# Six matmul widths instead of five in an expert loop, and its code on a block boundary

## What is computed

```python
logits = (xt @ router_w + router_b)                  # 1024 tokens x 32 experts
top_val, top_idx = lax.top_k(logits, 4)              # each token goes to 4 experts
# for the tokens of expert e (xb), in blocks:
gu  = xb @ w_gu[e] + b_gu[e]                         # 1024 -> 2048
act = glu * sigmoid(1.702 * glu) * (lin + 1)         # from the two halves of gu, clamped
y   = act @ w_down[e] + b_down[e]                    # 1024 -> 1024
# y times the token's gate is added to the token's row
```

```
139 138 60 61 114 114 145 77 129 120 134 122 117 149 116 80
80 128 217 110 143 174 181 168 118 161 168 117 108 184 156 68
```

## Time and profile before

| | |
|---|---|
| median of 3 executions | 2286.57 us (2285.47 to 2297.29) |
| profiled execution, its own time | 2288.99 us |
| its span, first to last instruction | 2287.2 us |
| TensorE matmul busy | 2216.6 us, 97% of the span |
| matmuls of the expert loop (L1031) | 1563.1 us busy, 12,288 of them |
| mean granted TensorE clock | 0.986 of full speed |

### The profile page before, as it was taken

How to read it: one execution, slowest core, us unless ns; L and a number is a source line. 1 busy time by engine, 2 the same in 40 slices (tenths; PEclk the granted TensorE clock), 3 DMA queues, 4 the chain that set the end, 5 groups by cost and what they waited for, 6 DMA issues and landing times.

```text
span 2287.2 us, 40244 instructions
## 1 busy us (share of the span) xinstructions
PE 2216.6 (97%) x14694; PEld 1904.5 (83%) x14695; DVE 1412.9 (62%) x2880; ACT 570.8 (25%) x1248; POOL 259.4 (11%) x237
## 2 busy tenths in 40 slices
PE   8999999999987999999999999999999999999996
PEld 4444554556667999999999999999999999999996
DVE  3442231577765687768767767764765566667567
ACT  2122221344401222222222222221222222222123
POOL 1000000021141011001101110010110010000013
PEclk9999999999988999999999999999999999999998
DMA  8000002111145899989989889885987788788788
GB/s 310 33 0 1 0 1 74 72 56 57 47 142 187 266 313 300 311 272 316 314 278 304 293 261 318 303 284 188 316 252 235 238 264 291 247 289 297 236 253 295
DMA packets 244509, 486.79 MB, mean 213 GB/s; under 512 B 24552, under 2 KB 24760, under 8 KB 244428
## 3 DMA queue, kind: packets, MB, share of 16 engines
q1 hardware_dynamic: 223532, 450.36, 56.7%
q0 software_dynamic: 20704, 35.60, 7.2%
q10 hardware_dynamic: 224, 0.16, 0.0%
HBM read 475.57 MB, written 49.61 MB: 230 GB/s over the span
## 4 chain that ended last, share of the span: by engine, by line
PE 92%; DVE 4%; issue 2%; ACT 1%; DMA 1%; POOL 0%; DVEq 0%; SPq 0%; POOLq 0%; ACTq 0%
PE PS L1031 65%; PE PS L662 15%; PE PS L858 5%; PE PS L798 1%; PE PS L831 1%; DVE pairA L1807 1%; PE PS L820 1%; PE PS L743 1%; PE PS L740 0%; PE PS L877 0%; DVE unit L1536 0%; PE PS L635 0%; DVE pairA L1853 0%; PE PS L698 0%; DMA unit<-h_dram,cur_x 0%
## 5 line engine op out<-in xcount | busy, mean ns | idle before, releaser
L1031 PE MATMUL PS<-pairA,unit 128*128 x12288 | 1563.1, 290 | 32.9 <-issue 29.1
L1031 PEld LDWEIGHTS PS<-pairA,unit 128*128 128x128 f32 x12288 | 1554.6, 191 | 41.6 <-issue 41.0
L1788 DVE STREAM_TRANSPOSE unit<-unit 32x512 f32<-32x512 f32 (+1 forms) x512 | 325.5, 636 | 10.9 <-DMA unit<-h_dram,cur_x 3.7
L1807 DVE STREAM_TRANSPOSE pairA<-unit 32x512 f32<-32x512 f32 (+1 forms) x512 | 325.8, 636 | 7.1
L662 PE MATMUL PS<-pairA,unit 128*128 128x512 f32 (+1 forms) x528 | 233.6, 598 | 1.6 <-issue 1.6
L1290 ACT ACTIVATE unit<-PS,cur_b 128x256 f32<-128x256 f32 x256 | 107.5, 471 | 408.0 <-PE PS L1031 408.0
L558 POOL DMA_INDIRECT unit<-h_dram,cur_x x66 | 68.8, 1042 | 1186.0 <-DVE cur_x L1843 1162.4
L662 PEld LDWEIGHTS PS<-pairA,unit 128*128 128x128 f32 (+1 forms) x528 | 97.7, 189 | 119.0 <-issue 118.2
L1273 ACT ACTIVATE unit<-unit 128x512 f32<-128x512 f32 x128 | 80.6, 630 | 461.8 <-DVE unit L1835 461.8
L1279 ACT ACTIVATE unit<-PS,cur_b 128x256 f32<-128x256 f32 x256 | 107.5, 471 | 318.8 <-PE PS L1031 315.3
L1827 DVE COPY cur_b<-b_all 128x24 f32 x32 | 6.7, 209 | 258.4 <-ACT unit L1290 254.5
(11 more groups left out here) (257 smaller groups left out, 1171.9 us busy)
## 6 DMA issues: line engine op xcount, KB each, us to landing
unit<-in_expert_w_gu_dram SPq DMA_DIRECT2D x256, 1024.0 KB, 5.0
unit<-in_expert_w_down_dram SPq DMA_DIRECT2D x128, 1024.0 KB, 8.4
unit<-in_w_in_dram SPq DMA_DIRECT2D x6, 2048.0 KB, 16.1
pairB<-in_x_dram SPq DMA_DIRECT2D x16, 512.0 KB, 6.1
unit<-in_w_out_dram SPq DMA_DIRECT2D x2, 2048.0 KB, 8.6
h_dram<-pairA SPq DMA_DIRECT2D x8, 512.0 KB, 2.6
acc_dram<-pairB SPq DMA_DIRECT2D x8, 512.0 KB
pairB<-acc_dram SPq DMA_DIRECT2D x8, 512.0 KB, 8.0
```

Source lines behind the costliest of these rows:

```text
L1031: ins = pe.matmul(ps[:, ITEM * (j % 2):ITEM * (j % 2) + w], slot_w[s][:, k, P * j:P * j + P], xa_cols[:, ITEM * kd:ITEM * kd + KD * ITEM + ...
L1788: ins = dve.transpose(cols[:, :, :, 32 * q:32 * q + 32], rows[:, :, :, 32 * a:32 * a + 32])
L1807: ins = dve.transpose(rows[:, :, :, 32 * a:32 * a + 32], cols[:, :, :, 32 * q:32 * q + 32])
```

## The change

The list of widths gets six entries, 128 to 224, so that by the counts above 17 items take 128 columns, 4 take 140 (items 0, 1, 8, 10), 3 take 152 (6, 13, 20), 4 take 168 (23, 25, 26, 30), 3 take 184 and one 224. `by_width` then tests n > 128, n > 152, and on the wide side n > 168 and n > 184, on the other n > 140. Ahead of the loop an alignment directive asks that TensorE's next instruction stands at a multiple of 256 instructions. The loop for extra items behind it, with the one width CAP, is not touched.

```diff
@@ -53,7 +53,7 @@
 LISTS = 2 * (ROUNDS + 1)
 CAP_BITS = 21
 CAP_MUL = (1 << CAP_BITS) // CAP + 1
-WIDTHS = [132, 148, 168, 184, CAP]
+WIDTHS = [128, 140, 152, 168, 184, CAP]
 SLOTS = 4
 NO_ROW = 1 << 20
 
@@ -1050,6 +1050,7 @@
                                                yT[:, 4 * side + m, P * (q // 2):P * (q // 2) + P], ident[:, :])
                         ins.then_inc(y_ps, 1)
 
+            pe.addr_align(256)
             with pe.Fori(0, 3 * N_EXP):
                 one_pass(WIDTHS)
             pe.wait_ge(items_ready, 2)
```

## The result

The kernel with six widths on a block boundary takes 2319.04 us (median of 6 executions, 2306.43 to 2326.76) against 2286.92 us for the kernel before (6 executions, 2284.26 to 2297.29). The ratio is 1.0135, 95% interval 1.0117 to 1.0153: slower by 1.35%, 32 us. The prediction was 2272.5 us, 0.6% faster, with a range up to 2283. The profiled execution took 2321.7 us, with a span of 2319.9.

The account below looks back on a forecast made before the run. TensorE's stream of weight loads and matmuls was taken to bound the loop. -12.5 + 0.4 - 4.0 + 1 + 1 = -14.1 us gave 2272.5 us, 0.6% less than the median of 2286.57; range 2261 to 2283 us.

Parts of the forecast that it names:

- The bound: Expert loop: worth what TensorE's stream of weight loads and matmuls takes, with PE busy 97% of the span.
- The step that decides: Loop matmuls of 128 columns: weight load sets a 111.7 ns pace, 0.8 ns less than at 132; 5.4 us saved.
- Rival 1: Loop matmuls of 128 columns: columns set the pace, 109.2 ns, giving 2259 us; chance 0.05.
- The widths: Loop items at their new widths: gains and losses over the 32 items sum to -12.5 us.
- rival 4: Change of pass: branch costs eat the widths' gain, 140 sitting behind two taken branches; chance 0.17 together with another rival.
- Behind wide items: Items 19, 24, 27, 31, each behind a wide one: lose some 0.1 us each to weights, +0.4 us.
- The start: First passes of the loop, item 0: both 1.9 us jump stalls go, -4.0 us, bounds 0 and -8.
- the padding: Slots ahead of the loop, at most 255: +1 us, 0.2 if jumped over, 4.5 at most if run through.
- The program's place: Loop's instruction blocks: 1,630 instructions, kept by the alignment on no more than 7 blocks.
- a single miss: Width whose block item 0 never touched: may miss once at its first turn; +1 us taken, up to +5.
- Rival 2: Loop no longer stays resident, far branches of 5 us return: 2430 us or more; chance 0.09.

Follow-up runs that it names:

- e8: Against e3, widths 100, 132, 168, 184, 224 in place of 132, 148, 168, 184, 224; 2316.25 us in its one execution.
- e12: Against e11, only the order of width tests changed: n > 128, then n > 168; 2263.35 us.
- e2: Kernel before with its five widths, plus the alignment, padding run through as no-ops; 2269.90 us.
- e10: The changed kernel unchanged, run again for a second trace; 2322.69 us.
- e5: Kernel before with its five widths, the loop begun at slot 232 of a block, 30 slots later, padding jumped over; 2290.05 us.
- e11: The changed kernel with its alignment padding jumped over instead of run through; 2318.74 us.
- e7: Against e4, the widths tested one after the other from the narrowest up; 2275.79 us.
- e6: Kernel before plus a sixth width, 188, that no item takes, aligned, padding jumped over; 2296.39 us.
- e4: Against e3, the two narrowest of five widths changed from 132 and 148 to 130 and 145; 2261.81 us.
- e3: Kernel before with its five widths, plus the alignment with padding jumped over; 2268.22 us.

## Why the prediction was wrong

**The bound: right.** The loop is still worth what TensorE's stream takes, and nothing waits for weights by name.

**The step that decides, the pace of 128 columns: right.** Matmuls, and so weight loads, start 111.6 to 111.7 ns apart in the first passes of 128-column items, and the window is 43.40 us. Rival 1 (109.2 ns) falls. e8 settles it: 100 columns give the same 43.40 us. The Trainium skill ("TensorE: Matmul & The Clock Gate", LDWEIGHTS) would have a load take 107 ns; these runs show 111.7 for fp32.

**The widths: right.** Over items 2 to 17 the terms came to -6.8 us, and -6.2 were measured, with 47.3 and 50.5 us for 140 and 152 columns. The branches of rival 4 cost what they did before. e8 shows that its mechanism is real: there 132-column items took 1.7 us more behind a second taken branch. The change put none ahead of its narrowest body.

**Behind wide items: +0.4 us was too little.** Without stalls, in e12, items 19, 24, 27 and 31 took 44.3, 44.4, 43.8 and 43.5 us, together 2.4 us over four times 43.4; in the kernel before they were 0.8 us over four times 43.7. So the term measures +1.6 us. And the waits that the trace names there, 0.5 us in item 19 and 0.7 in item 24, are for VectorE's `actT` (L1854), not for weights. The rows that I read the 0.4 us from name no wait for weights either.

**The start: right in direction, far too small.** I took -4.0 (bounds 0 and -8) and +1 for the padding. The padding was run through in 6.5 us, outside its bound of 4.5; in e2 and e10 it took 4.0, inside it, so the +1 was too low either way, and what is over is three no-ops of 0.6 to 0.7 us in this one execution. Against that, both long jumps went, and of the four long branches of L974 those of pass 1 went altogether: 27.1 us of long branches became 8.2, and the passes of item 0 behind them ran nearer to full speed: 18.4, 15.5 and 15.5 us at 140 columns, where 15.5 is the full speed, after 19.4, 18.0 and 18.0 at 148, where it is 16.4. Six packets came from 663 to 735 us, where I expected 12 to 15. Up to item 2 the difference is -16.8 = 2.9 (the part ahead of the loop) + 6.5 (padding) - 4.8 (widths of items 0 and 1, as forecast) - 21.4 (the rest, mostly the stalls). e2 measures the alignment alone, padding included, at -17.9 by the medians.

**The program's place: the step that failed.** It read "The alignment therefore keeps it on no more than 7" blocks, and took that as enough to stay resident, because the kernel before does so on 6 or 7. The cost of a block that item 0 never touched was booked as a single miss: "I take +1, up to +5". It measured some +56 us (55.6 in items 19 to 31, where the widths gave -0.9). The first late packet comes at 1515.9 us, 18 us into item 18, which is the first to take the 224 body. That body ends at 1.13, so I read the packet as block 2, fetched ahead when the sequencer came to block 1. From item 20 on, branches that had not missed for 900 us miss again and again. I had even noted the fact that should have priced this: every body of the kernel before first ran without a fetch. I put that down to room. It was because item 0 had happened to bring in all blocks, by landing at 2.96 and not at 3.08; e5 moves it by 30 slots, and two stalls appear.

**Rival 2 was the nearest**, with 0.09. It said that the loop no longer stays resident. Its sign and its "three missed branches in all" were right: there were nine. Its price of 2430 us or more was not, as it supposed misses in every item. And its cause, seven blocks being too many, is refuted by e12, whose loop lies on the same seven and ran 1,500 us with no fetch. The Trainium skill ("Runtime: NRT & Kernel Launch", Instruction fetch mechanics) says that a taken branch out of a two-page window forces a fetch. e12 shows otherwise: of its 210 width branches from 741 us on, the taken ones from block 0 to block 2 or 5 among them, none took over 210 ns, and no packet came. It also calls the store first-in, first-out, which no run here decides.

**Without the late stalls** the time lies inside the range: e12, with its padding jumped over, gives 2263.35 us, 9 less than forecast. That it comes so near is partly luck. In its trace item 2 starts 24.4 us earlier than in the kernel before, where the forecast had 7.8, and items 2 to 31 save only 1.8 us, where the forecast had 6.3: besides the wide items, its order of tests puts 152 columns behind two taken branches (51.1 us an item in place of 50.5).

**What stays open.** That the late stalls cost the time is shown by e11 against e12. That they go with a block first loaded late is shown by the seven traces against the eight, and by the quiet stretch that each of the seven has from item 1 to its first late packet; before against e5 is the smallest pair, with two stalls. But an order of tests that brings block 2 in early also sends later items back to it: in e12 every item of 140 to 168 columns tests n > 140 there. No run loads the block early and then leaves it alone, so whether the early load or the later visits keep the loop quiet isn't separated. That e7 had no more stalls behind item 13, though its 145-column items still go past block 2, speaks for the load. Which block is given up, by what rule, and why the misses mostly come in pairs in successive passes, I can't say, and I have no rule that gives the changed kernel's 9, e6's 5 and e7's 3. Executions of the changed kernel spread over 20 us and those of e12 over 1.7, so the number of stalls may well differ from one to the next. Nor is it explained why the kernel before fetched in pass 1 what pass 0 had just fetched.

## What to carry to other kernels

Where a TensorE loop of several 16 KB blocks picks one of many bodies, what counted here, up to 7 blocks, was less its size than that its first passes touched every block; order the branches so that they do, and look for instruction packets in the middle of the loop, not only around its start. A page on which PE is 97% busy before and 96% after hides this; the waits named "issue", split by stretch, and the longest branch in each stretch show it. And count such a stall of TensorE at about one and a half times its length, for the clock behind it: here 36.3 us of idle time brought 16.6 us of longer passes.

## What the runs showed of the hardware

- A loop of 1,630 instructions on 7 blocks of 256 ran 1,500 us with no instruction packet (e12). A far width branch that missed took 3.3 to 7.2 us with its fetch, a taken one without a fetch 202 to 210 ns in e12 from 735 us on.
- With 128 x 128 fp32 weights the matmul's pace is 111.5 to 111.7 ns at 100 (e8), 128 (the changed kernel) and 130 columns (e4) alike, and 112.5 ns at 132.
- Eight of the nine late stalls of the changed kernel were followed by a longer pass, by 1.3 to 2.7 us, the granted clock being 0.59 in the mean of 6.6 us behind one of them. The ninth, ahead of pass 24.0, left PE idle for 2.46 us, and that pass took 14.55 us, 0.1 more than in e12.
- 54 no-ops of padding took 4.0 us in two traces (e2, e10) and 6.5 in one. Jumping over them gained 1.7 us by the medians with five widths (e3) and 0.3 with six (e11).
